# Fifteen of the 32 experts of a mixture-of-experts layer in blocks of 64 tokens

## The reference

```
gt  = min(xb @ w_gate[e] + b_gate[e], 7)
up  = clip(xb @ w_up[e] + b_up[e], -7, 7)
hdn = (up + 1) * gt * sigmoid(1.702 * gt)
y   = hdn @ w_down[e] + b_down[e]        # then times the token's gate, summed per token
```

## Time and profile before

| | |
|---|---|
| median of 3 runs | 1453.19 us |
| profiled execution | 1450.85 us |
| its span (first to last instruction) | 1448.9 us |
| mean granted TensorE clock | 0.980 |
| PE busy | 1387.8 us, 96% |
| DVE (VectorE) busy | 1270.5 us, 88% |
| ACT (ScalarE) busy | 966.5 us, 67% |
| POOL (GpSimd) busy | 189.6 us, 13% |
| DMA | 479.55 MB, mean 331 GB/s |

### The profile page before, as it was taken

One profiled execution on the slowest core, in us unless ns is written; L12 is line 12 of the kernel. 1 busy time (PEld: TensorE's weight loads), 2 busy tenths in 40 slices (PEclk: granted clock), 3 DMA queues, 4 the chain that ended last, 5 costly groups with the idle time before them and its releaser, 6 DMA issues.

```text
span 1448.9 us, 18708 instructions
## 1 busy us (share of the span) xinstructions
PE 1387.8 (96%) x6456; PEld 1146.7 (79%) x6456; DVE 1270.5 (88%) x996; ACT 966.5 (67%) x740; POOL 189.6 (13%) x191
## 2 busy tenths in 40 slices
PE   5999989799999999999999999999999999999994
PEld 4887767678888888888888888888888888888874
DVE  6899855899888888888888888888888888888898
ACT  3132643467777777777777777777777777777761
POOL 3000000011111111111111111111111111111062
PEclk9999789899999999999999999999999999999997
DMA  9922302799999999999999999999999999999983
GB/s 295 337 60 76 128 1 77 271 408 377 384 394 384 383 388 387 374 390 389 373 392 392 385 385 378 382 384 387 385 382 384 388 384 381 397 381 378 404 308 103
DMA packets 84978, 479.55 MB, mean 331 GB/s; under 512 B 10731, under 2 KB 11030, under 8 KB 35798
## 3 DMA queue, kind: packets, MB, share of 16 engines
q1 hardware_dynamic: 71982, 433.40, 76.8%
q0 software_dynamic: 6944, 25.18, 5.0%
q10 hardware_dynamic: 6024, 20.60, 3.6%
HBM read 449.82 MB, written 29.33 MB: 331 GB/s over the span
## 4 chain that ended last, share of the span: by engine, by line
PE 86%; DVE 9%; ACT 1%; issue 1%; DMA 1%; POOL 0%; SPq 0%; POOLq 0%; DVEq 0%; ACTq 0%
PE pair L1747 23%; PE pair L1745 23%; PE pair L1746 23%; DVE area_m L1016 2%; PE pair L1732 2%; PE pair L1725 2%; PE pair L1758 2%; PE pair L1530 2%; PE pair L1531 1%; PE pair L1532 1%; DVE w_low L1170 1%; DVE win_low L991 1%; DVE h L1443 1%; DMA h<-in_x 1%; PE pair L1611 1%
## 5 line engine op out<-in xcount | busy, mean ns | idle before, releaser
L1170 DVE TENSOR_TENSOR w_low<-w_raw,w_high 128x2048 fp32r<-128x2048 f32 x380 | 863.9, 2289 | 108.9 <-ACT w_high L774 105.8
L774 ACT CAST w_high<-w_raw 128x2048 fp32r<-128x2048 f32 x380 | 727.8, 1916 | 279.6 <-PE pair L1747 278.3
L1745 PE MATMUL pair<-w_high,xT_high 128*128 128x512 f32 x1008 | 395.1, 392 | 0.5 <-DVE xT_low L1228 0.5
L1747 PE MATMUL pair<-w_high,xT_low 128*128 128x512 f32 x1008 | 393.0, 390 | 0.0
L1746 PE MATMUL pair<-w_low,xT_high 128*128 128x512 f32 x1008 | 392.4, 389 | 0.0
L1747 PEld LDWEIGHTS pair<-w_high,xT_low 128*128 128x128 f32 x1008 | 189.2, 188 | 39.6
L1745 PEld LDWEIGHTS pair<-w_high,xT_high 128*128 128x128 f32 x1008 | 189.3, 188 | 39.2 <-DVE xT_low L1228 0.9
L1746 PEld LDWEIGHTS pair<-w_low,xT_high 128*128 128x128 f32 x1008 | 189.3, 188 | 38.4
L1745 PE MATMUL pair<-w_high,hT_high 128*128 128x512 f32 x496 | 195.8, 395 | 0.0
L1747 PE MATMUL pair<-w_high,hT_low 128*128 128x512 f32 x496 | 193.3, 390 | 0.0
L1746 PE MATMUL pair<-w_low,hT_high 128*128 128x512 f32 x496 | 193.3, 390 | 0.0
(11 more groups left out here) (300 smaller groups left out, 1399.6 us busy)
## 6 DMA issues: line engine op xcount, KB each, us to landing
w_raw<-in_w_gate SPq DMA_DIRECT2D x128, 1024.0 KB, 7.0
w_raw<-in_w_up SPq DMA_DIRECT2D x128, 1024.0 KB, 6.5
w_raw<-in_w_down SPq DMA_DIRECT2D x128, 1024.0 KB, 7.0
y_rows<-area_m ACTq DMA_DIRECT2D x30, 512.0 KB, 7.6
ring<-in_w_in SPq DMA_DIRECT2D x5, 2048.0 KB, 17.7
y_rows<-area_t SPq DMA_DIRECT2D x1, 8704.0 KB, 37.0
ring<-in_w_out SPq DMA_DIRECT2D x2, 2048.0 KB, 8.5
h<-in_x SPq DMA_DIRECT2D x4, 512.0 KB, 8.7
```

Source lines behind the costliest of these rows:

```text
L774: s.copy(w_high[:, i % HIGH_RING, :], w_raw[i][:, :]).then_inc(high_ready, 1)
L1170: v.tensor_tensor(w_low[i][:, :], w_raw[i][:, :], w_high[:, i % HIGH_RING, :].bitcast(F32), ALU.subtract).then_inc(low_ready, 1)
L1745: t.matmul(to[half], tok_high, hi, start=(opens and kk == 0), stop=False)
L1747: last = t.matmul(to[half], tok_low, hi, start=False, stop=(k == KD - 1))
```

## The change

On the chip the experts are ordered by their token counts. Expert 0 stays at place 0. The fifteen smallest of the others take the places 1, 3, ..., 29; the other sixteen take the even places from 2 and place 31. The block at an odd place up to 29 is small: it holds at most 64 tokens, in rows 64 to 127, and the count and the ranks of its expert are raised by 64 for that.

In a small block the low and the high rows (64 each) lie side by side as one stationary matrix of 128 columns. It is multiplied with the high weights and with the low weights: 8 matmuls for a piece in place of 12. PSUM rows 64 to 127 then hold the high products, rows 0 to 63 the low ones. To add them, ScalarE copies rows 0 to 63 to SBUF after the last piece of the product, while the next product is under way, (`fold_copy`), and TensorE adds them to rows 64 to 127 with a 64-row matrix `shift_down` (`fold`, two matmuls of 512 columns). That is done three times for a small block, for gate, up and down. (The low weights also multiply the low rows, which adds a product that was left out before.)

SyncE and GpSimd read the expert's number of a place from the table `order`. Half of the `y_rows` of the small blocks (3.9 MB) is filled with zeros by one DMA, early in the kernel: SyncE issues it behind the eight loads from which VectorE makes the first two of the eight attention bias tables (L1037), and ahead of the loads for the next two.

The core of the diff:

```
+            def piece_small(i, at, both, to, opens=False):
+                pe.wait_ge(low_ready, at + 1)
+                for kk in range(KPP):
+                    k = KPP * (i % 4) + kk
+                    rows = both[:, k, :, :].rearrange("p a t -> p (a t)")
+                    for half in range(2):
+                        cols = slice(kk * D_MODEL + half * HALF, kk * D_MODEL + (half + 1) * HALF)
+                        t.matmul(to[half], rows, w_high[:, i % HIGH_RING, cols], start=(opens and kk == 0), stop=False)
+                        last = t.matmul(to[half], rows, w_low[i][:, cols], start=False, stop=(k == KD - 1))
+                last.then_inc(piece_used, 1)
+            def fold(rows, to, count):
+                pe.wait_ge(fold_copied, count)
+                for half in range(2):
+                    last = t.matmul(to[half], shift_down[:, :], rows[:, half * HALF:(half + 1) * HALF], start=False, stop=True,
+                                    skip_group_check=True)
+                last.then_inc(folded, 1)
...
+            def pe_even(j, h):
+                base = PIECES * j + 8
+                gate(j + 1, base, turn=j, small=True, fold_down=None if isinstance(j, int) and j == 0 else 3 * h)
+                up(j + 1, base + UP, small=True, fold_gate=3 * h + 1)
+                pe.wait_ge(hT_low_ready, j + 1)
+                transpose_x(j + 2)
+                down(j, base + DOWN, fold_up=3 * h + 2)
+            def pe_odd(j):
+                base = PIECES * j + 8
+                gate(j + 1, base, turn=j)
+                up(j + 1, base + UP)
+                pe.wait_ge(hT_low_ready, j + 1)
+                transpose_x(j + 2)
+                down(j, base + DOWN, small=True)
...
+            def xS_low_part(b):
+                dve.wait_ge(xT_high_ready, b + 1)
+                v.tensor_tensor(xS[:, :, 0, :], turned_small(), xS[:, :, 1, :].bitcast(F32), ALU.subtract).then_inc(xT_low_ready, 1)
+            def fold_copy(to, of, at):
+                act.wait_ge(piece_used, at)
+                s.copy(to[:, :], of[0:SMALL, :]).then_inc(fold_copied, 1)
...
+                if pair == 0:
+                    halves = y_rows[0:LATE * CAP, :].rearrange("(m s i) (j f) -> (i j) m s f", s=4, i=SMALL, f=HALF)[:, :, 2, :]
+                    sp.dma_start(halves, zeros.unsqueeze(1).to_broadcast([P, LATE // 2, HALF])).then_inc(halves_zeroed, 16)
```

The ordering is new work on VectorE, between the count and the table of tokens, and one small matmul:

```
+            then(v.scalar_tensor_tensor(key, counts[:, :], float(N_EXPERTS), iota_f[:, 0:N_EXPERTS], ALU.mult, ALU.add))
...
+            then(v.tensor_scalar(key_junk, key, key_col, None, ALU.is_lt))
+            then(v.tensor_reduce(n_below, key_junk, AX.X, ALU.add))
...
+            dve.wait_ge(sorted_turned, 1)
...
-            then(v.tensor_tensor(picked, exp_1h, across(first_extra[:, :], NJ), ALU.mult))
-            then(v.tensor_reduce(first_j[:, :], picked, AX.X, ALU.add))
+            then(v.scalar_tensor_tensor(place_off, first_extra[:, :], 32.0 * 1024, place_off, ALU.mult, ALU.add))
...
+            then(v.tensor_copy(packed_i[:, :], packed_f))
```

More of the change, by code:

```diff
@@ L36 @@
 CAP = 128
+SMALL = CAP // 2
 EXTRA = (SEQ - 1) // CAP
@@ L244, in encoder_kernel @@
         before_b = sb("before_b", [P, P], BF16)
-        colT = sb("colT", [P, 32])
+        colT, col_at = area("colT", [P, 32])
+        order = over("order", col_at, 0, [P, N_EXPERTS], I32)
         convT = sb("convT", [P, P])
@@ L486, in reload, with expert_at @@
                 load(i, e)
+            def expert_at(b):
+                return sp.value_load(order[0:1, bass.ds(b, 1)], min_val=0, max_val=N_EXPERTS - 1)
+            sp.wait_ge(order_ready, 1)
+            second = expert_at(1)
             for i in range(GATE, DOWN):
@@ new lines, in _ @@
+            v.tensor_scalar(sorted_rhs[:, 1, :], ident[:, 0:N_EXPERTS], is_small, None, ALU.mult)
+            v.tensor_scalar(sorted_rhs[:, 2, :], iota_f[:, 0:N_EXPERTS], place, c_flt[:, 2:3], ALU.is_equal, ALU.mult).then_inc(sorted_ready, 1)
+            then(v.tensor_copy(rank_place, bank[0][:, 0:NQ * 32].rearrange("p (n e) -> p n e", n=NQ)))
+            dve.wait_ge(sorted_turned, 1)
+            place_row, small_row, order_row = (bank[4][:, 32 * i:32 * i + 32] for i in range(3))
+            v.tensor_copy(order[:, :], order_row).then_inc(order_ready, 1)
@@ L1776, in gate, with up, down @@
                         between()
-            def up(b, base, high=xT_high, low=xT_low, between=None):
+            def up(b, base, high=xT_high, low=xT_low, between=None, fold_gate=None, small=False):
                 if not (isinstance(b, int) and b == 0):
                     pe.wait_ge(u_limited, b)
-                add_bias(U_TO, sel_up, bias_gu)
+                add_bias(U_TO, half_up if small else sel_up, bias_gu)
                 for i in range(4):
-                    piece(UP + i, base + i, high, low, U_TO)
+                    if small:
+                        piece_small(UP + i, base + i, xS, U_TO)
+                    else:
+                        piece(UP + i, base + i, high, low, U_TO)
+                    if i == 1 and fold_gate is not None:
+                        fold(fold_g, G_TO, fold_gate)
                     if i == 1 and between is not None:
                         between()
-            def down(b, base, place=DOWN, to=D_TO, turn=None, unstored=0, high=hT_high, low=hT_low):
+            def down(b, base, place=DOWN, to=D_TO, turn=None, unstored=0, high=hT_high, low=hT_low, fold_up=None, small=False):
                 pe.wait_ge(hT_low_ready, b + 1)
@@ L1794, in down @@
                 for i in range(4):
-                    piece(place + i, base + i, high, low, to, opens=(i == 0))
+                    if small:
+                        piece_small(place + i, base + i, hS, to, opens=(i == 0))
+                    else:
+                        piece(place + i, base + i, high, low, to, opens=(i == 0))
+                    if i == 1 and fold_up is not None:
+                        fold(fold_u, U_TO, fold_up)
                     if i == 1 and turn is not None:
                         transpose_h(turn)
-            def pe_pass(j):
+            def pe_even(j, h):
+                base = PIECES * j + 8
+                gate(j + 1, base, turn=j, small=True, fold_down=None if isinstance(j, int) and j == 0 else 3 * h)
[4 more added lines that the diff above has]
+            def pe_odd(j):
                 base = PIECES * j + 8
@@ L1804, in pe_pass @@
                 transpose_x(j + 2)
-                down(j, base + DOWN)
+                down(j, base + DOWN, small=True)
             transpose_x(0)
```

260 lines of the change are left out of this document (200 added, 60 removed).

## The result

The changed kernel takes 1376.19 us, the median of 4 runs (1371.91 to 1377.44), against 1454.6 us of the kernel before on the same chip. The ratio is 0.9461, with a 95% interval of 0.944 to 0.9483. The forecast was 1375 us. The profiled execution took 1371.91 us, 78.9 us less than that of before; it is the shortest of the four.

What follows compares the result with a forecast made beforehand. TensorE sets the pace, with DMA and VectorE close behind; a pair goes from 70.76 to 65.0 us. Loop -84, routing +4.5, zeros +0.5, end +0.5 give -78.5 us: from 1453.2 to 1375 us, range 1351 to 1417.

Steps and rivals of the forecast that it cites:

- the first pair: Early expert loop, where VectorE is the bound already: half a pair's gain counted, so 14.5 x 5.8 = 84 us in all.
- TensorE's work: Expert loop: matmuls dropped, folds added; TensorE's work for a pair of passes goes from 70.76 to 62.5 us.
- The price of going into 64 rows: At each fold, going into a 64-row matmul and out costs 0.39 us, three times a pair 1.2 us.
- the lead: VectorE's lead entering the small stretch, 4.0 us, against 4.2 us lacking there; pair 62.7 us if carried, 66.7 if not.
- two ends of 65.0 us: Pair of passes: 65.0 us, the middle of DMA's 63.5 (421 GB/s) and VectorE's 66.7; DMA rate near 411 GB/s.
- DMA is the bound: Rival in the expert loop: DMA stays at its present busy rate, 68.0 us a pair, 1417 us; chance 22%.
- all lead kept: Rival in the expert loop: VectorE's lead carries over wholly, DMA holds 421 GB/s, pair 63.5 us, 1353 us; chance 10%.
- The rival of 358 GB/s: Expert loop: DMA falls to the HBM limit, pair 74.7 us, 59 us more, 1518 us; chance 1%.
- The ordering: Ahead of the first expert: about 23 small VectorE operations cost 4.6 us, moving the first tokens' subtraction by 4.5 us.
- The zeros: Early tables: 3.9 MB at 421 GB/s take 9.3 us, nearly covered, costing 0.5 us; 8 us at half the rate.
- The clock: Rival in small stretches: TensorE's waits lower its clock, 1690 us at worst; chance 5%. Below 1.00 in the loop is wrong.
- The extra block: Rival after the last block: a small block overflows 64 tokens, over 80 us; chance 4% including an unseen stall.

Runs made afterwards that it cites:

- The extreme case: Changed kernel with both moves, the fold at 128 rows and half of w_low for small pieces, with full or cut stores: 1350.4 and 1362.86 us, one run each.
- the 128-row fold: Changed kernel with shift_down and the copied rows widened to 128 rows, 64 of them multiplied by zeros: 1361.83 us, ratio 0.9371.
- a move: Changed kernel with one operation later: hidden by one subtraction (1367.27 us, ratio 0.9403), or rows_out_small behind the gate fold's copy (1366.81 us, ratio 0.9398).
- all is moved: Changed kernel with hidden and rows_out_small later, the fold at 128 rows and zeros two pairs of tables later: 1361.97 us, ratio 0.9359.
- thin stores: Only 64 of 1024 columns of each output row stored, on the kernel with all three edits: 1391.61 us; with half of w_low for small pieces too: 1362.86 us.
- run with half of VectorE's work: Changed kernel where the subtraction for small-block pieces makes only the first 1024 of 2048 w_low columns, used twice: 1352.31 us, one run.
- the run with fourteen: Changed kernel with the order turned round, so the largest experts take small places and fourteen extra blocks run: 2216.37 us, one run.

## Why the prediction was right

**The sum.** Measured between the same points of the two profiled executions: the front is 4.7 us longer (forecast 4.5 + 0.5). From the subtraction of the first tokens to the last one of its kind (1365.90 before, 1288.11 after) are 1087.65 us before and 1005.13 after, 82.5 less (forecast 84). The rest is 0.9 us shorter (forecast 0.5 longer). That is -78.7 us, against -78.5. The medians are 78.4 us apart. An agreement to 0.2 us is luck: the four runs of the changed kernel spread over 5.5 us, the profiled one is the shortest, and its front is shorter than in any of the later runs with the same front. Of the gain in the loop, the 14 pairs between the stores of blocks 0 and 28 give 990.82 - 909.53 = 81.3 us, and the first pass 1.4, where the forecast gave the first pair 2.9.

**TensorE's work.** Forecast 62.5 us for a pair, measured 62.9 between the waits. The extreme case is nearer still: 61.6 us where nothing holds TensorE and the fold has 128 rows, plus the 0.99 of the 64 rows, are 62.6. The other 0.3 us fit the steps made longer by late weight loads; no run put that to the test alone. The price of going into 64 rows, 0.39 us from one place of the trace of before, is 0.41 for one fold of the loop and 0.3 for the two others, 1.0 us a pair where the forecast had 1.2, and the 128-row fold shows the cause. The forecast had seen the price in the kernel before without asking whether it could be avoided at once.

**VectorE and the lead.** The step of the forecast was that the small stretch needs more of VectorE than of TensorE, and that the lead carries an unknown part of the 4.2 us. The small stretch, from 763.63 to 791.53 in TensorE's timeline, takes 27.9 us: 25.9 of work and 2.0 of waits. With the transposes right behind it it is 28.7, and the full stretch has the other 36.3 us, as forecast. Only 1.15 us of the waits are VectorE's, so about three quarters of the 4.2 us were carried. The small pieces therefore don't step by 2.3 us as forecast. They step by 1.82 us, eight matmuls, and one wait among the twelve takes what VectorE lacks. A full piece steps by 829.94 - 827.21 = 2.73 us, as forecast. Two things were off: VectorE's pair without its listed waits is 65.0 - 2.7 = 62.3 us, not 60.8 (part of that are gaps too short for the list: four subtractions at 784.40 take 9.07 us, and 8.89 elsewhere), and part of TensorE's waits came from the order (the fold's copy behind `rows_out_small`, `hidden` in the same piece as two others), which the forecast did not look at. The experiments show that order and amount of work both count: a move gives 0.65 us, and when all is moved, VectorE has no idle time left around the small stretch and the pair stops at 63.9. It still waits 2.3 us a pair for ScalarE among the full pieces, where the time is of no use to it.

**DMA.** It was chosen as one of two ends of 65.0 us, at a rate near 411 GB/s. The rate came out at 411, but as a demand: 26.7 MB in the 64.97 us that the engines need. Its limit is 415 GB/s and 64.4 us, seen only when all else was faster. The optimistic end of 421 GB/s was the rate of 35 us, and no stretch of 130 us in the loop held it in the runs that were pushed to the limit, with thin stores no more than with full ones. So the rival "DMA is the bound" fell, by only 0.6 us. The rival "all lead kept" fell too: TensorE still waits 2.0 us in a pair. Its pair of 63.5 us is below DMA's own. The run with half of VectorE's work held 63.47 us to the end of the loop, but only out of the reserve in `w_raw`. The rival of 358 GB/s, which rests on the Trainium skill's page DMA: Bandwidth & Descriptors, fell far: 411 GB/s held over 700 us.

**Ahead of the loop.** The ordering was sized at 4.6 us of VectorE's small operations; it took 280.77 - 263.05 = 17.7 us from the mark at 263.05, where before it was 13.8, so 3.9. Alone, with the zeros, it made the kernel 4.4 us slower (2.6 to 6.0), against 5.0 forecast. The zeros were mis-sized: 0.5 us forecast, 2.3 us of waits for the tables' loads measured. They landed 12.7 us after their issue, some 310 GB/s, where the forecast took 421. At 263.05 the changed kernel is only 1.1 us behind. But with the same front this mark lies at up to 266.46 in the later runs, so how much of the zeros' cost arrives there is not settled.

**The clock.** From 400 us on it stayed at 1.00, as forecast, with a wait of 1.2 us and one of 0.9 in each pair. In the first pass it did not, and the forecast had named that as a sign of being wrong. TensorE's transposes at 320.60 had waited 2.49 us for `hidden`; right behind them matmuls step by 0.42 us instead of 0.227, as at the lower level in the earlier trace rows, and the busy time by stage has 0.89.
```profile
320.00:335.00 15.00, 14.40 (x60) 11.67 (x61) 14.79 (x14) 11.10 (x9) 3.77 (x2) 0.89 0.88 346
```

By the step times that cost one or two us, once; the kernel before has no such dip in its loop. In the extra blocks, with waits of up to 6.8 us, the clock fell to 0.83.

**The extra block.** No small block had more than 64 tokens. Had one, the price would have been, by an estimate from the run with fourteen, 56 + 52 = 108 us, and the kernel would have been some 30 us slower than before. The forecast's "over 80 us" named both parts, the block at 50 us and the gathers at 30 or more, and had both too small. Its reason for the 50 was wrong: ScalarE and VectorE overlap within a product, and the time goes between the products.

Two signs that the forecast named did not come: the small pieces' step of 2.3 us, and the clock that stays at 1.00 through the whole loop. The choice of the middle between two ends had luck in it: the value came out, but from 62.9 us of TensorE's work and two waits of about 1 us, and not from DMA.

## What to carry to other kernels

When a change takes work off the bounding engine, work out the second engine's time for each stretch, not for the whole loop, and count how much lead the buffers allow; then look at which of its operations stand together where the stretch begins. A transfer limit just behind shows in landing times that grow from stretch to stretch, long before any engine waits for a transfer; so read the pair's time at the end of the loop and not only at its start. Where a matmul needs only 64 rows of contraction between matmuls of 128, padding it with zeros to 128 was free here and won 0.3 to 0.4 us each time. Before you price an overflow path from a run, count in the trace how often it ran, and tell the part that comes each time from the part that comes once.

## What the runs showed of the hardware

GpSimd's small casts of `is_expert` took up to 9.0 us. Groups by line in the changed kernel (500 to 1200 us), then in the run with half of VectorE's work and in the 128-row fold alone (500 to 1150 us); before, the first of the two casts took 1.10 us on average and the second 0.29.
```profile
L612 POOL CAST sel_gate<-is_expert 128x128 fp32r x11 | 49.3, 4480 | 180.8 <-PE pair L1939 180.8
```
```profile
L612 POOL CAST sel_gate<-is_expert 128x128 fp32r x10 | 2.9, 292 | 160.4 <-PE pair L1949 160.4
```
```profile
L613 POOL CAST sel_up<-is_expert 128x128 fp32r x10 | 90.3, 9029 | 0.0
```

The operation is the same size each time. In the changed kernel the second cast takes 2.35 us. Beside VectorE's timeline the cause is plain. A cast that meets no subtraction takes 0.29 us, as in the run with half of VectorE's work, whose edit touches nothing of GpSimd's. A cast that starts during a `w_low` subtraction lasts until VectorE leaves a gap behind one: in the 128-row fold alone it starts at 842.84, four subtractions follow each other by 2.20 us, the last of them starts at 849.43 and ends at 851.71, the next starts only at 851.73, and the cast ends at 851.86. Beside `hT_low_part`, which reads one of its inputs from PSUM, a cast keeps its 0.29 us (`hidden` one piece later, 782.71 within 782.41 to 783.63). So GpSimd's cast is held as long as VectorE's subtractions, which have both inputs in SBUF, run without a gap. That the place of the inputs is what matters rests on these two kinds of operation alone. It costs nothing here: GpSimd is busy 19% of the span, and nothing waits for it.
